# Turned V taken first in its step, with earlier splits, transposes and loads around it, in a neighbourhood-attention encoder layer

## The reference, cut to what matters

```
qkv = x @ w_qkv                       # 16 heads of 64
s   = q k^T / 8 + rpb                 # a window of 8 rows x 16 columns around each query
out = softmax(s) @ v
x   = layer_norm(2**0.25 * x + out @ w_o)
hid = square(relu(x @ w_ff1));  ple = sigmoid(x @ w_gate) * (p @ w_proj)
x   = layer_norm(2**0.25 * x + hid @ w_ff2 + ple)
```

## Time and profile before

| what | value |
|---|---|
| device time, median of 3 runs | 1227.69 us (1227.55 to 1228.03) |
| device time of the profiled execution | 1227.37 us |
| its span, first to last instruction | 1225.5 us, granted TensorE clock 0.999 |
| TensorE busy, weight load busy | 1214.2 us (99%), 1019.7 us (83%) |
| VectorE, ScalarE, GpSimd busy | 879.1 (72%), 593.7 (48%), 108.2 us (9%) |

### The profile page before, as it was taken

How to read it: one execution, slowest core, us unless ns; L and a number is a source line. 1 busy time by engine, 2 the same in 40 slices (tenths; PEclk the granted TensorE clock), 3 DMA queues, 4 the chain that set the end, 5 groups by cost and what they waited for, 6 DMA issues and landing times.

```text
span 1225.5 us, 17905 instructions
## 1 busy us (share of the span) xinstructions
PE 1214.2 (99%) x5820; PEld 1019.7 (83%) x5820; DVE 879.1 (72%) x1740; ACT 593.7 (48%) x1145; POOL 108.2 (9%) x73
## 2 busy tenths in 40 slices
PE   9999999999999999999999999999999999999997
PEld 7888888888888888888888888888888888888886
DVE  3677777777777857769777777777764575588786
ACT  3555655655556843244544454444453433333671
POOL 0212222122123014200000000000000000000000
PEclk9999999999999999999999999999999999999999
DMA  8323223212232757683666565565579876768633
GB/s 219 78 72 77 58 72 90 55 55 72 57 106 83 272 158 227 201 284 129 197 206 232 175 230 206 190 238 178 220 237 379 282 273 226 254 236 311 195 103 103
DMA packets 162694, 215.61 MB, mean 176 GB/s; under 512 B 11456, under 2 KB 91200, under 8 KB 162240
## 3 DMA queue, kind: packets, MB, share of 16 engines
q1 hardware_dynamic: 162624, 214.72, 53.9%
HBM read 147.57 MB, written 58.90 MB: 168 GB/s over the span
## 4 chain that ended last, share of the span: by engine, by line
PE 96%; DVE 2%; ACT 1%; issue 1%; DMA 0%; DVEq 0%; ACTq 0%; SPq 0%
PE bank L2733 25%; PE bank L2701 25%; PE bank L1183 18%; PE bank L1334 7%; PE bank L2657 6%; PE bank L1286 3%; PE bank L1263 3%; PE bank L1242 3%; PE bank L1218 2%; PE bank L1325 1%; PE bank L1197 1%; PE bank L257 1%; PE bank L1234 1%; DMA x_chunk<-in_x 0%; DVE k_lo_twice L1036 0%
## 5 line engine op out<-in xcount | busy, mean ns | idle before, releaser
L867 ACT ACTIVATE probabilities<-negated_scores,negated_max 128x384 f32<-128x384 f32 (+1 forms) x128 | 75.6, 591 | 135.6 <-DVE negated_max L1070 135.2
L1183 PE MATMUL bank<-act_T_hi,w_qkv_hi 128*128 128x512 f32 x336 | 133.7, 398 | 0.0
L1183 PE MATMUL bank<-act_T_lo,w_qkv_hi 128*128 128x512 f32 x336 | 133.5, 397 | 0.0
L1183 PE MATMUL bank<-act_T_hi,w_qkv_lo 128*128 128x512 f32 x336 | 131.8, 392 | 0.0
L2701 PE MATMUL bank<-x_combination,weight_parts 128*128 128x512 f32 x504 | 118.5, 389 | 0.0
L1051 DVE TENSOR_TENSOR prob_T_lo<-bank,prob_T_hi 128x256 fp32r<-128x256 f32 (+2 forms) x160 | 69.0, 448 | 59.1 <-ACT prob_T_hi L858 57.5
L2701 PEld LDWEIGHTS bank<-x_combination,weight_parts 128*128 128x128 f32 x504 | 94.6, 188 | 19.6
L2701 PE MATMUL bank<-act_T_hi,weight_parts 128*128 128x512 f32 x240 | 77.3, 389 | 0.0
L2061 ACT ACTIVATE hidden_staging<-hidden_staging 128x512 f32<-128x512 f32 x48 | 30.4, 632 | 94.9 <-DVE hidden_staging L2398 94.9
L752 POOL TENSOR_TENSOR w_qkv_lo<-weight_raw,w_qkv_hi 128x1024 fp32r<-128x1024 f32 x21 | 50.3, 2394 | 282.2 <-ACT w_qkv_hi L813 282.2
L2733 PE MATMUL bank<-x_combination,hidden_parts_odd 128*128 128x512 f32 (+1 forms) x324 | 73.1, 381 | 0.0
(11 more groups left out here) (262 smaller groups left out, 2806.0 us busy)
## 6 DMA issues: line engine op xcount, KB each, us to landing
hidden_combinations<-hidden_staging SPq DMA_DIRECT2D x112, 256.0 KB, 2.6
w_ff_in<-in_w_ff SPq DMA_DIRECT2D x27, 1024.0 KB, 8.1
weight_raw<-in_w_ff SPq DMA_DIRECT2D x25, 1024.0 KB, 5.5
weight_raw<-hidden_combinations SPq DMA_DIRECT2D x14, 1024.0 KB, 5.5
hidden_in<-hidden_combinations SPq DMA_DIRECT2D x14, 1024.0 KB, 5.8
weight_raw<-in_na_w_qkv SPq DMA_DIRECT2D x21, 512.0 KB, 4.4
bias_in<-rpb_rows SPq DMA_DIRECT2D x256, 6.0 KB
attention_T<-out_T SPq DMA_DIRECT2D x8, 512.0 KB, 2.9
```

What stands on the lines that cost most here:

```text
L867: nc.scalar.activation(prob[:, u % 4, 0:n], score[:, u % 2, 0:n], ACT.Exp, scale=-1.0, bias=nmax[:, u % 4:u % 4 + 1], accum_out=total[:, u ...
L1183: mm = nc.tensor.matmul(proj_ps[gi % 2][:, :], w[wp][:, (par + kind) % 2, k, :], S.act[ap][:, k, t * HALF:(t + 1) * HALF], start=(i == 0), ...
```

## The change

It has five parts. (a) In the seven pairs with projections `turned_v` becomes the first thing of steps 5 and 8 on both engines: before `turned_tile` on ScalarE, before `normalise` and `turned_tile` on VectorE. (b) In the first stage, the second half of chunk 0 is copied by VectorE and no longer by ScalarE, the halves of chunk 1 are both transposed behind the third product of the second pass, ScalarE splits the weights of chunk 0 after the first half of x, and from chunk 2 on both engines split the weights before x; chunk 1 of x has a semaphore of its own. (c) One of the transposes of p moves from step 17 to step 18. (d) In the last pair the splits of w_o and of the two early tiles are spread out (steps 1, 3, 5, 7, 9, 11 for 1, 2, 4, 5, 7, 8, and 12 and 14 for 10 and 12), their loads follow, and the early products begin at step 15 in another order, with the same fourteen blocks in all. (e) The attention output of tiles 2 and 3 is loaded in two pieces, seven pairs early and the last pair from SBUF, ahead of the store.

```diff
-P_TURN_STEP = (17, 17, 17, 18)
+P_TURN_STEP = (17, 17, 18, 18)
-WO_SPLIT_STEP = (1, 2, 4, 5, 7, 8, 16, 17)
-WO_LOAD_STEP = {4: 4, 5: 5, 7: 6, 8: 7}
-EARLY_SPLIT_STEP = (10, 12)
+WO_SPLIT_STEP = (1, 3, 5, 7, 9, 11, 16, 17)
+WO_LOAD_STEP = {4: 4, 6: 5, 8: 6, 10: 7}
+EARLY_SPLIT_STEP = (12, 14)
-EARLY_PRODUCTS = {16: 2, 17: 3, 18: 3, 19: 3, 20: 3}
+EARLY_PRODUCTS = {15: 2, 16: 2, 17: 2, 18: 3, 19: 3, 20: 2}
+EARLY_ORDER = [(0, 0), (1, 0), (0, 1), (1, 1)] + [(k, h) for k in range(2, KC) for h in range(2)]
...
@@ SyncE, body and tile
+                if not more:
+                    sp.wait_ge(score_full, UNITS * PAIRS)
+                    for i in range(2):
+                        sp.dma_start(o_raw[:, i, 0:LAST, :],
+                                     bass.AP(S.oT.tensor, (2 + i) * P, [[T, P], [P * T, LAST], [1, P]])).then_inc(o_in[i], 16)
...
+                    for i in range(2):
+                        sp.dma_start(o_raw[:, i, LAST, :], o_st[:, (2 + i) * P:(3 + i) * P]).then_inc(o_in[i], 16)
...
@@ ScalarE, first stage
-            for k in range(KC):
+            x_high(0, 0)
+            first_split(0)
+            x_high(1, 0)
+            x_high(1, 1)
+            first_split(1)
+            for k in range(2, KC):
+                first_split(k)
                 x_high(k, 0)
                 x_high(k, 1)
-                first_split(k)
...
@@ ScalarE, body
+                    if more and s - 1 in V_TURN_STEP:
+                        turned_v(1 - par, j + 1, V_TURN_STEP.index(s - 1))
                     if PARTS <= s < UNITS + PARTS:
                         turned_tile(j, s - PARTS)
...
-                    if more and s - 1 in V_TURN_STEP:
-                        turned_v(1 - par, j + 1, V_TURN_STEP.index(s - 1))
...
@@ VectorE, first stage
+            def first_copy():
+                dve.wait_ge(x_turned, 2)
+                nc.vector.tensor_copy(x_dest(0, 0, 1), x_chunk_T(1)).then_inc(first_q, 1)
...
+            first_copy()
-            for k in range(KC):
+            for k in range(2):
                 x_low(k, 0)
                 x_low(k, 1)
                 first_split(k)
+            for k in range(2, KC):
+                first_split(k)
+                x_low(k, 0)
+                x_low(k, 1)
...
@@ TensorE, first stage
-                    if n == 1:
-                        turn_x(1, t)
+                    if n == 1 and t == 0:
+                        for half in range(2):
+                            turn_x(1, half)
```

More of the change, by code:

```diff
@@ L403, in attention @@
         early_in = [sem(f"attention_early_in{t}") for t in range(2)]
-        ln_in = sem("ln1_in")
+        second_in = ln_in = sem("second_x_chunk_in_then_ln1_in")
         o_in = [sem(f"attention_tile_in{i}") for i in range(2)]
@@ L499, in chunk_there, with x_highs @@
         def chunk_there(k):
-            return chunk_in[k % 4], 16 if k == 0 else 32 if k < 4 else 48 if k == 4 else 64
+            return chunk_in[k % 4], 16 if k < 2 else 32 if k < 4 else 48 if k < 6 else 64
+        def x_highs(k, t):
+            return 1 if k == 0 else 2 * k + t
         def first_raw(kind, k):
@@ L710, in tile @@
                     load_x(0, 0)
-                    load_attention(2, 0)
                     sp.wait_ge(o_lo, 2 + 2)
+                    sp.wait_ge(out_stored, 16 * (PAIRS + 1))
+                    for i in range(2):
+                        sp.wait_ge(o_in[i], 32)
                     load_x(1, 1)
-                    load_attention(3, 1)
                     return
@@ L968, in split @@
             def split(t, par, nth):
-                act.wait_ge(o_in[par], 16 * nth)
+                act.wait_ge(o_in[par], 16 * (nth + 1))
                 act.wait_ge(y_full, 2 * t + 2)
@@ L1015, in first_split @@
                                             first_w(0, kind)[:, k, :].bitcast(F32), ALU.subtract).then_inc(first_lo, 1)
+            def first_copy():
+                dve.wait_ge(x_turned, 2)
+                nc.vector.tensor_copy(x_dest(0, 0, 1), x_chunk_T(1)).then_inc(first_q, 1)
             def x_low(k, t):
-                dve.wait_ge(x_hi, 2 * k + t + 1)
+                if k == 0 and t:
+                    dve.wait_ge(first_q, 2)
+                else:
+                    dve.wait_ge(x_hi, x_highs(k, t))
                 nc.vector.tensor_tensor(x_dest(1, k, t), x_chunk_T(t), x_dest(0, k, t).bitcast(F32),
@@ L1143, in _ @@
             pairs_loop(dve, body)
-            dve.wait_ge(ln_in, 32)
+            dve.wait_ge(ln_in, 16 + 32)
             def tile(t, par, nth):
@@ L1191, in turn_x @@
                     pe.wait_ge(x_first_in, 16)
+                elif k == 1:
+                    pe.wait_ge(second_in, 16)
                 else:
@@ L1210, in first_products @@
                 else:
-                    pe.wait_ge(x_hi, 2 * k + 2)
+                    pe.wait_ge(x_hi, x_highs(k, 1))
+                    pe.wait_ge(first_q, 2)
                 if 2 in passes:
@@ L1252, in scores @@
                     pe.wait_ge(k_doubled, 64 * j + 64)
-                    pe.wait_ge(first_q, 1 + 1)
+                    pe.wait_ge(first_q, 2 + 1)
                 if u == 3:
@@ L1257, in scores @@
                     pe.wait_ge(proj_free, 6 * j + (6 + 2))
-                    pe.wait_ge(first_q, 1 + 2)
+                    pe.wait_ge(first_q, 2 + 2)
                 pe.wait_ge(score_done, UNITS * j + (u + 1))
@@ L1339, in early_products @@
             def early_products(t, first, last):
-                for k, h in [(k, h) for k in range(KC) for h in range(2)][first:last]:
+                for k, h in EARLY_ORDER[first:last]:
                     if k == 0 and h == 0:
```

9 lines of the change are left out of this document (3 added, 6 removed).

## The result

The changed kernel takes 1231.83 us (median of 7 runs, 1230.91 to 1232.21), the kernel before 1227.69 us on the same chips (7 runs): a ratio of 1.0033, 95% interval 1.0023 to 1.0043. It is slower by 4.1 us. The profiled executions have spans of 1229.4 and 1225.5 us, 3.9 us apart. In the changed kernel's listing `turn_p`'s transposes are L1275 (L1242 before), the low part of the turned probabilities L1076 (L1051), `add_bias` L1095 (L1070), `normalise` L1102 and L1104 (L1077, L1079), V's high and low part L859 and L1068, the scores L1296 (L1263).

The account below looks back on a forecast made before the run. TensorE was taken as the bound, busy all but 11.3 us. On the profiled 1227.37 us, 5.7 - 0.45 + 0 - 1.0 = +4.25 gave 1231.6; the runs' median, 0.32 higher, made it 1231.9, stated as 1232.0, range 1226.1 to 1233.7.

Parts of the forecast that it names:

- Part (a): V turned first in the seven pairs: 7 x 0.83 less about 0.1, 5.7 us slower, bounds 2.8 and 7.0.
- the ring: In each pair `add_bias`, exponential, high part, low part and next `add_bias` release one another; a delay passes on unchanged.
- the wait for V's high part: Step 5: VectorE waits for ScalarE until 210.52, `normalise` and the low part queued behind; `add_bias` comes 0.78 us late.
- the cover at step 9: `add_bias` of step 9 waited for scores anyway, which covers 0.66 of the 1.49 us delay; 0.83 stays.
- step 16: TensorE has no slack before these transposes, so it idles about 0.8 us there in each of seven pairs.
- `normalise` at 0.66 us: Length of `normalise` at step 5 (207.68 to 208.34), one term in the 0.78 us delay of `add_bias`.
- Part (b): First stage: chunk 1's first product waits less because both halves of x are turned earlier; -0.45 us, bounds 0 and -0.48.
- from chunk 2 on nothing waited: First stage: no wait stood behind chunk 1, so no gain or loss was counted there.
- Part (c): Third transpose of p stops waiting 0.4 us, but the fourth waits at step 18: 0, bounds +0.1 and -0.7.
- Part (d): Last pair: spread splits free one wait and early products cover another; -1.0 us, bounds -1.4 and +0.8.
- the upper bound of +0.8: Last pair: nothing freed, and one split of 0.9 us exposed.
- the rival of the lock: `normalise` at step 10 runs into GpSimd's split, 1.9 us more in each of seven pairs, 1245 us; chance 0.03.

Follow-up runs that it names:

- undo_a: The changed kernel with both engines' turned V back in its old place: 1227.92 us (10 runs), ratio to before 1.0002.
- vector_only: The changed kernel with ScalarE's turned V back behind the evacuations, so only VectorE takes V first: 1237.04 us.
- scalar_only: The changed kernel with VectorE's turned V back behind the low part, so only ScalarE takes V first: 1229.62 us.
- v_low_third: The changed kernel with VectorE's turned V behind `normalise` and ahead of the probabilities' low part, ScalarE taking V first: 1227.38 us (10 runs), ratio 0.9999.
- chunk1_back: v_order_and_start with the halves of x's chunk 1 turned as before the change: 43.12 us from first product to first scores, against 42.44.
- v_order_and_start: The same kernel as last_pair_back, timed in more rounds: 1226.21 us (11 runs), ratio to before 0.9993.
- low_in_pieces: v_low_third with GpSimd's low part of each early attention tile as seven instructions instead of one: last pair 72.42 us, against 73.13.
- split_back: v_low_third with the early attention splits back in steps 10 and 12 of the last pair: last pair 73.09 us.
- wo_ten: v_low_third with the sixth w_o split in step 10 of the last pair instead of step 11: last pair 73.12 us.
- last_pair_back: v_low_third with the last pair's w_o splits and loads, early splits and early products as before the change, early loads kept: last pair 72.52 us.
- before_again: The kernel before, profiled once more: first product at 7.45 us, first scores 43.40 us behind it.

## Why the prediction was right, and where it was off

**Part (a), the mechanism: right.** It named the ring, the wait for V's high part with `normalise` queued behind it, the cover at step 9, and step 16 as the place where TensorE pays; the trace shows each, seven times, and undo_a removes all of it. The idle before the transposes of step 16 was foretold as 0.8 us and the pairs as 50.3; they came 0.5 us later and 50.03 to 50.07.

**Part (a), the size: 4.0 us, not 5.7.** The term that was mis-sized is `normalise` at 0.66 us (207.68 to 208.34). That is the distance to the next instruction's start, and it held 0.14 us of waiting for ScalarE's high part, which ran from 207.92 to 208.30 in the same timeline. Where nothing waits, `normalise` occupies 212.31 to 212.83, 0.52 us. Counted twice a pair: 0.83 - 2 x 0.14 = 0.55, and the six later pairs measured 0.49 to 0.57. The first pair was counted like the others and cost 0.79: there the wait for scores at step 9 covers 0.36 (`add_bias` 1.17 late at step 8, 0.81 at step 9) and not 0.65. Vector_only and scalar_only, sized with 0.52 and ScalarE's 0.48 us for V's high part, came out at 1.35 and 0.31 a pair where 1.35 and 0.30 had been worked out.

**The cover at step 9: right.** In the fourth pair `add_bias` is 1.17 us late at step 8 and 0.52 at step 9 in the changed kernel, 0.94 and 0.28 in scalar_only, 2.01 and 1.36 in vector_only: 0.65 or 0.66 covered each time, where 0.66 was said. v_low_third has it 0.15 late at step 8 and on time at step 9, and its pairs are as long as before.

**Part (b): right at chunk 1, wrong behind it.** 0.48 us at chunk 1 was foretold as 0.45, and chunk1_back gives it back. But "from chunk 2 on nothing waited" was carried over to the new order without asking what the weights' low parts, now ahead of x's, would meet: in the changed kernel one met GpSimd's bias, and TensorE lost 0.41 us at chunk 7, so that little of the 0.48 is left. In v_order_and_start and v_low_third, with the same order of the start, this wait is absent. That the profile gained 0.70 all the same is luck: 0.39 us come from the first product and 0.13 from the second, by the pace of TensorE's first products, which changes from one execution of a kernel to the next.

**Part (c): 0, right.** The wait moved to the fourth transpose, 0.4 us of TensorE at 398.14.

**Part (d): the sign was wrong, 1.6 us off.** -1.0 was said, +0.56 came, inside the upper bound of +0.8 but by another mechanism than that bound's. The step that failed is that moved splits were costed as work on ScalarE alone. Each early split has a low part of 2.1 us on GpSimd, each w_o split one of 1.2 us on VectorE, and the rival of the lock was worked out for step 10 of the pairs only, not for the last pair, whose GpSimd instructions were what moved. The hold is worth 0.7 us of the 1.6 (low_in_pieces). The other 0.9 is a gain that didn't come: the wait before the transposes at 434.66 is gone as foretold, 0.70 us by start-to-start times, but where before had 0.38 at 410.07, low_in_pieces loses 0.33 and 0.26 at its steps 6 and 7, 0.23 at step 13 and 0.32 at an early product, 1.4 us in the whole last pair against 1.5. Why the spread splits bring these back, no run takes apart.

**The sum.** 4.02 + 0.56 - 0.70 = 3.88 against +4.25: two errors of 1.7 and 1.6 us with opposite signs, and a third of 0.25 at the start. The total of 1232.0 against 1231.83 is nearer than its parts deserve.

## What to carry to other kernels

Before an instruction that waits for another engine is moved forward, list what is queued behind it, and ask of each whether it used to run inside that wait: here 0.52 us of `normalise` lost its cover twice a pair, and with `normalise` in front of the wait the same move of V costs nothing.

Take an instruction's occupancy from a place where the next one waits for nothing; start to start where something waits overstates it.

When a split moves, its second half on the other engine moves too: lay its new interval over every VectorE instruction there which GpSimd can hold (in these traces those that read and write only SBUF), and look in the stage where it goes, not only where it was.

## What the runs showed of the hardware

GpSimd's instruction holds a VectorE TENSOR_SCALAR from SBUF to SBUF that begins inside it until it has ended (1.60 to 1.68 us instead of 0.42 in the last pair of after, v_low_third and split_back), and in seven pieces it doesn't (0.43). A TENSOR_SCALAR that begins just ahead of GpSimd isn't held (428.44 against 428.65 in wo_ten; 0.43 us at most in 20 such places of the fourteen profiles).

A VectorE TENSOR_TENSOR with both operands in SBUF is held too: 128x128 takes 0.28 us, but 1.12 us inside the bias building of after (36.39), and 2.47 or 2.48 between 31 and 33 us in each of the eleven profiles with the new start in which GpSimd's low part of w_qkv is one instruction. With one operand in PSUM it isn't: the probabilities' low part of 128x256 keeps its 0.42 to 0.43 us in 224 places inside a GpSimd instruction, K's low part its 0.69 to 0.70 us in 196.

Each further piece costs GpSimd 0.14 to 0.19 us: 3.10 us for seven where one took 2.12, 2.83 and 2.95 for four where one took 2.41 and 2.39.

The eight idle products at the start take 1.91 or 1.92 us in the profiles of before, before_again and undo_a, and 1.06 or 1.07 us in those of after, v_low_third and last_pair_back, with a granted clock of 1.00 (the level of 2.4 GHz) in these stretches of all six; what makes the difference isn't known.
